# Third mixer: token parts behind the rotations and the last pair's copies first; first mixer: compression weights in a place of their own

## The chip, the core and the metric

The kernel runs on one core of a Trainium2 chip. The metric is the device time of one execution in microseconds (us). Engines are named as in the profile: PE is TensorE (PEld its weight loads), DVE is VectorE, ACT is ScalarE, POOL is GpSimd, and SP is the sync engine, which issues the DMAs.

## What is computed

Two transformer layers with modulated norms, then a third block of another make, on one sequence of 256 tokens and width 1024, all in float32:

```python
for layer in range(2):
    shift, scale, gate = split(c @ mod_w[layer, 0] + mod_b[layer, 0], 3)
    h = rms_norm(x, w) * (1 + scale) + shift
    y = mixer_ab(h, ...) if layer % 2 == 0 else mixer_cd(h, ...)
    x = x + gate * rms_norm(y, w)
    ...                                   # the same around swiglu(h, w_in, w_out)
# first mixer (ab), NSA part: compressed keys and values
kc = einsum('bnlgd,lde->bnge', k_cmp[:, gidx] + cmp_pe, cmp_wk)
vc = einsum('bnlgd,lde->bnge', v_cmp[:, gidx] + cmp_pe, cmp_wv)
# ... compressed, selected and window attention, weighed by gates; and a sliding window attention with sinks
# third mixer (sb): attention with rotated q, k and a token MLP, side by side
attn = block_attention(rope(rmsnorm(q)), rope(rmsnorm(k)), v)
tok = u * (einsum('hpq,bcqhd->bcphd', w_s, rmsnorm(v_tok)) + b_s)
mixed = concatenate([rmsnorm(attn, g_attn_out), rmsnorm(tok, g_tok_out)])
x = x + gt1 * (mixed @ w_out)             # then a gated FFN with a 3-tap convolution, and a last norm
```

## The kernel before

The program is written out engine by engine, with semaphores between the engines; nothing schedules it but the order of the code. The activations lie transposed (features on the 128 partitions, 256 tokens along the row). Every product of a weight with activations is made of three matmuls of fp32r, on the high and low parts of both operands (`three`, L1990 to L1992): high by high, low by high, high by low. For that each weight **unit** of 128x1024 is loaded to `raw` (SP, `load_unit`, L650), its high part is written by ACT to `wH` (`split_high`, L810) and its low part by DVE to `wL` (`split_low`, L1276), in rings of six slots. Beside this DVE makes the modulation vectors (`do_job`, L627 and L629): one **product** per modulation tile of 128x1024, which SP loads to `modbuf` (`load_job`, L660). In the first mixer a tile may be loaded once the product two before it is done (`mod_used`).

The stages in order: start, first mixer (ab, to about 180 us), FFN f0, second mixer (cd), FFN f1, third mixer (sb, 740 to 837 us), FFN f2, last norm.

**First mixer.** After the projections of keys and values, a loop of 15 steps `s` runs on SP, ACT, DVE and PE, each with its own list. In steps 0 to 11 PE makes the scores of two heads (`ab_scores`, L2332, L2335). DVE adds the bias and takes the minimum (`ab_neg`, L1629, L1631), ACT takes the exponential (`ab_exp`, L1005, with sinks L1010 from step 8). One step later DVE makes the factors of the rows (`ab_weigh`, L1639 to L1646) and scales the later two thirds of each head's probabilities (L1651), ACT scales the first third (L1018); this is "the weighing of step s - 1". Then PE turns the probabilities (`ab_turn`, L2347), ACT copies them out of PSUM (`ab_take_pt`, L1025), PE multiplies them with the values (`ab_pv`, L2364, L2367), ACT takes the high part of the finished features (`ab_features_high`, L1034) and DVE the low part (`ab_features_low`, L1657). The heads are numbered b = 2s and 2s + 1. In each step PE also does one projection (`ab_project`), from step 9 on one or two output products of 24 matmuls (`ab_out`).

The NSA compression runs in steps 0 and 1: `compress` (L2277 for the keys, L2280 for the values) multiplies windows with the weights `cw`, which lie in `otok` (1 MB on chip). Key and value weights share that place, so SP waits for the key product before it loads the value weights (L714). In step 5 PE turns the compressed probabilities (L2455), ACT copies them to `pcT` (L1084), and PE waits for that copy before it turns head 9. The hot matmul for the compressed bias (`misc["bc"]`, L2402) reads `hot_cmp`, in `proj` 9 to 12, at about 49 to 50 us; those tiles of `proj` are written with projections from step 4 on. `acc0[:, 2D:3D]` is written by the products from step 9 on.

**Third mixer.** The attention runs in four pairs of heads: `rope(n)` rotates a tile (L1822 to L1829), `pair_scores` (L2602), `pair_max` (L1837), `exp_pair` (L1161), `pair_turn` (L2617), then the two copies out of PSUM, the first head's by DVE (`copy_first`, L1848) and the second head's by ACT (`copy_second`, L1173), then `pair_pv` (L2631). Both copies count on one semaphore, `pt_ready`, and `pair_pv` waits for both. Scores of pair t need rotation t + 1. The token half is split into high and low parts by `mix_high` (ACT, L1183) and `mix_low` (DVE, L1877), which `token_out` reads, four units later.

```python
            def pair_pv(t):                                # L2625, PE
                pe.wait_ge(pt_ready, 32 + 2 * t + 2)
...
            def copy_first(t):                             # L1842, DVE
...
                V.tensor_copy(pt[:, 0, :], bank[2][:, :]).then_inc(pt_ready, 1)
```

## Time and profile before

| what | value |
|---|---|
| three runs | 1047.26, 1046.67, 1045.31 us; median 1046.67 |
| profiled execution | 1044.85 us, of it 1043.1 us from the first to the last instruction |
| PE busy | 994.2 us (95%), 8118 matmuls |
| DVE busy | 793.6 us (76%) |
| ACT busy | 560.4 us (54%) |
| mean granted clock of PE | 0.985 |
| read from HBM | 225.04 MB |

PE is nearly always busy, so its idle stretches are few and can be listed one by one. Matmuls are pipelined, so the time of one (0.28 us) is longer than the distance between two (about 0.12 us at the full clock). An idle stretch is shown in brackets behind the instruction that ended it, with what released it. The granted clock is a share of 2.4 GHz.

### The profile page before, as it was taken

The numbers are of one execution on the slowest core, as the hardware profiler recorded it, in microseconds if no ns is written. First come the engines' busy times: TensorE is split into PE (matmuls) and PEld (weight loads), VectorE is DVE, ScalarE is ACT, GpSimd is POOL, SyncE is SP. The second block draws the span as 40 slices with busy tenths as digits, with TensorE's granted clock in tenths as the row PEclk, the third lists the DMA queues.
The fourth block names the chain that finished last, engine by engine and source line by source line (L and its number), as shares of the span: only waits on it lengthen the run. The fifth ranks groups of instructions, "written<-read, shape, count | busy, mean of one in ns | idle before, by whom it ended". The sixth has DMA issues, their size and how long they took to land. (4 is left out here: it accounts for less than half of the span.)

```text
span 1043.1 us, 21347 instructions
## 1 busy us (share of the span) xinstructions
PE 994.2 (95%) x8118; PEld 959.4 (92%) x8118; DVE 793.6 (76%) x1320; ACT 560.4 (54%) x1126; POOL 4.6 (0%) x14
## 2 busy tenths in 40 slices
PE   6999989999999999999999999999998999999995
PEld 5997768899999999989899999998988989999995
DVE  4757875798888777888778888877766758777775
ACT  2444764544444456564454444446656456776664
POOL 0100000000000000000000000000000000000000
PEclk9998998999999999999999999999998999999999
DMA  9967767288888665832648888775612325455531
GB/s 356 344 206 226 248 220 265 88 328 309 301 301 304 248 252 174 300 118 74 230 181 304 304 301 302 284 263 177 246 66 74 126 98 182 181 186 187 188 144 42
DMA packets 62409, 227.59 MB, mean 218 GB/s; under 512 B 7010, under 2 KB 7266, under 8 KB 61956
## 3 DMA queue, kind: packets, MB, share of 16 engines
q1 hardware_dynamic: 61556, 224.02, 59.7%
q0 software_dynamic: 640, 2.10, 0.8%
q8 instruction: 47, 0.77, 0.3%
q10 hardware_dynamic: 144, 0.52, 0.1%
q14 instruction: 22, 0.18, 0.1%
HBM read 225.04 MB, written 1.57 MB: 217 GB/s over the span
## 5 line engine op out<-in xcount | busy, mean ns | idle before, releaser
L1990 PE MATMUL bank<-hH,wH 128*128 128x258 f32 (+1 forms) x1544 | 444.5, 288 | 11.1 <-DVE hL L1341 8.1
L1991 PE MATMUL bank<-hL,wH 128*128 128x258 f32 (+1 forms) x1544 | 438.2, 284 | 0.0
L1992 PE MATMUL bank<-hH,wL 128*128 128x258 f32 (+1 forms) x1544 | 436.6, 283 | 0.0
L1276 DVE TENSOR_TENSOR wL<-raw,wH 128x1024 fp32r<-128x1024 f32 x270 | 328.1, 1221 | 44.7 <-ACT wH L810 43.5
L1990 PEld LDWEIGHTS bank<-hH,wH 128*128 128x128 f32 x1544 | 292.7, 190 | 19.2 <-issue 10.6
L810 ACT ACTIVATE wH<-raw 128x1024 fp32r<-128x1024 f32 x270 | 276.6, 1047 | 43.5 <-PE bank L1992 25.1
L1992 PEld LDWEIGHTS bank<-hH,wL 128*128 128x128 f32 x1544 | 293.9, 190 | 0.0
L1991 PEld LDWEIGHTS bank<-hL,wH 128*128 128x128 f32 x1544 | 293.4, 190 | 0.4
L1990 PE MATMUL bank<-aH,wH 128*128 128x256 f32 x592 | 170.6, 288 | 3.0 <-DVE wL L1276 3.0
L1991 PE MATMUL bank<-aL,wH 128*128 128x256 f32 x592 | 169.7, 287 | 0.0
L1992 PE MATMUL bank<-aH,wL 128*128 128x256 f32 x592 | 169.6, 287 | 0.0
L1990 PEld LDWEIGHTS bank<-aH,wH 128*128 128x128 f32 x592 | 115.9, 196 | 4.2 <-DVE wL L1276 3.2
L1991 PEld LDWEIGHTS bank<-aL,wH 128*128 128x128 f32 x592 | 115.9, 196 | 0.0
L1992 PEld LDWEIGHTS bank<-aH,wL 128*128 128x128 f32 x592 | 115.7, 195 | 0.0
L930 ACT ACTIVATE fcol<-bank 128x1 f32<-128x1 f32 x132 | 15.2, 166 | 136.5 <-PE bank L1992 136.4
L1508 DVE TENSOR_TENSOR sn<-bank,rstd 128x256 f32<-128x256 f32 x44 | 18.7, 425 | 51.7 <-ACT fcol L930 51.7
L962 ACT ACTIVATE aH<-sn 128x256 fp32r<-128x256 f32 x66 | 27.5, 417 | 48.9 <-PE bank L1992 25.0
L629 DVE SCALAR_TENSOR_TENSOR acc<-modbuf,par,acc 128x1024 f32<-128x1024 f32 x28 | 35.9, 1281 | 10.0 <-DMA modbuf<-in_mod_w 9.2
L1528 DVE SCALAR_TENSOR_TENSOR pr<-sq,par,pr 128x255 f32<-128x255 f32 x44 | 19.4, 481 | 29.9 <-ACT pr L948 29.9
L935 ACT ACTIVATE sn<-sn,fcol 128x256 f32<-128x256 f32 x44 | 22.4, 510 | 28.2 <-DVE sn L1508 28.2
L856 ACT ACTIVATE hH<-x,sc 128x256 fp32r<-128x256 f32 x40 | 18.6, 502 | 23.8 <-DVE x L1385 17.2
L944 ACT ACTIVATE sq<-sq,fcol 128x256 f32<-128x256 f32 x44 | 20.1, 503 | 21.0 <-DVE sq L1519 21.0
(351 smaller groups left out, 1144.0 us busy)
## 6 DMA issues: line engine op xcount, KB each, us to landing
raw<-in_weights SPq DMA_DIRECT2D x270, 512.0 KB, 4.6
modbuf<-in_mod_w SPq DMA_DIRECT2D x69, 512.0 KB, 6.1
modbuf<-in_w_ada SPq DMA_DIRECT2D x36, 512.0 KB, 6.2
strips<-in_mod_w SPq DMA_DIRECT2D x16, 512.0 KB, 7.1
strips<-in_w_ada SPq DMA_DIRECT2D x12, 512.0 KB, 6.9
strips<-bias_table POOLq DMA_DIRECT2D x8, 256.0 KB, 7.2
otok<-in_cmp_w SPq DMA_DIRECT2D x4, 512.0 KB, 8.7
raw<-in_mod_w SPq DMA_DIRECT2D x2, 512.0 KB, 5.0
```

What stands on the lines that cost most here:

```text
L629: ops.scalar_tensor_tensor(out=dst, in0=src, scalar=cc[:, k:k + 1], in1=dst, op0=ALU.mult, op1=ALU.add).then_inc(mod_used, 1)
L810: nc.scalar.activation(wH[:, slot, :], raw[:, slot, :], ACT.Copy).then_inc(hi_ready[c], 1)
L856: nc.scalar.activation(hH[:, k, 0:S], x[:, k, :], ACT.Copy, scale=sc1[:, a, k:k + 1]).then_inc(hH_ready, 1)
L935: nc.scalar.activation(sn[:, t % 2, 0:S], sn[:, t % 2, 0:S], ACT.Silu, bias=fcol[:, t % 2, 0:1]).then_inc(silu_ready, 1)
L944: last = nc.scalar.activation(z, z, ACT.Identity, bias=fcol[:, t % 2, n:n + 1])
L962: nc.scalar.activation(aH[:, t % 2, :], sn[:, t % 2, S:2 * S], ACT.Copy).then_inc(aH_ready, 1)
L1276: V.tensor_tensor(wL[:, slot, :], raw[:, slot, :], wH[:, slot, :].bitcast(F32), ALU.subtract).then_inc(lo_ready[c], 1)
L1508: V.tensor_tensor(sn[:, t % 2, 0:S], gate_bank[:, 0:S], rstd[:, :], ALU.mult).then_inc(g_scaled, 1)
L1528: chain.inc(V.scalar_tensor_tensor(out=dst[:, 1:S], in0=z[:, 0:S - 1], scalar=row[:, 4 * n:4 * n + 1], in1=dst[:, 1:S], op0=ALU.mult, op1= ...
L1990: mm(out, lhs_h, rhs_h, start=start, stop=False, skip_group_check=True)
L1991: mm(out, lhs_h, rhs_l, start=False, stop=False, skip_group_check=True)
L1992: return mm(out, lhs_l, rhs_h, start=False, stop=stop, skip_group_check=True)
```

## The change

In words:

- First mixer, weights: the value weights are no longer loaded to `otok` behind the key product, but in two halves to `proj` 9 to 12 and to `acc0[:, 2D:3D]`, four DMAs of 256 KB on SP's queue after a wait for the bias product, ahead of units 12 and 13. `compress` waits for 96 in place of 64 and reads the halves. 
- First mixer, ACT: the copy to `pcT` in step 5 goes ahead of the split and the exponentials; in steps 9 to 12 the split goes ahead of the copy `ab_take_pt(2s - 2)`.
- First mixer, DVE: a step ends with one product less where it had two, and the other one comes in the next step right behind the weighing, ahead of the low part and the scores.
- Third mixer: `mix_high` 0 and 1 go behind the two roots `qk_rs` 3 and 4, `mix_low` 0 and 1 behind the rotations 3 and 4 and the maximum of pair 2. The last pair's copies go ahead of a split on either engine. The two copies count on a semaphore each (`turned_copied`), and the products of each head wait for its own.

```diff
@@ build_program
+        cw_values = [t.rearrange("p (l e) -> p l e", e=HD)
+                     for t in (proj[:, 9:13, :].rearrange("p a s -> p (a s)"), acc0[:, 2 * D:3 * D])]
+        turned_copied = [sem(f"turned_copied{j}") for j in range(2)]
@@ SP
             jobs_upto(JOBS_END["start"] + 2)
+            sp.wait_ge(misc_psum, misc["bc"] + 1)
+            for n in range(2):
+                for g in range(G):
+                    sp.dma_start(cw_values[n][g * HD:(g + 1) * HD],
+                                 A["cmp_w"][1][:, n * CLEN // 2:(n + 1) * CLEN // 2]).then_inc(cw_landed, 16)
             for p in range(12, 14):
                 load_unit(p)
             for s in range(AB_STEPS):
-                if s == 1:
-
-                    sp.wait_ge(misc_psum, misc["cmpk"] + 1)
-                    for g in range(G):
-                        sp.dma_start(cw[g * HD:(g + 1) * HD], A["cmp_w"][1]).then_inc(cw_landed, 16)
@@ ACT, first mixer
                     ab_weigh(s - 1)
+                if s == 5:
+                    act.wait_ge(pcT_psum, 1)
+                    nc.scalar.activation(pcT, bank[3][:, 0:S].rearrange("p (q n) -> p q n", q=QT),
+                                         ACT.Copy).then_inc(pcT_ready, 1)
...
+                split_upto(ab_split(s))
                 if 9 <= s <= 12:
                     ab_take_pt(2 * s - 2)
-                split_upto(ab_split(s))
...
-                if s == 5:
-                    act.wait_ge(pcT_psum, 1)
-                    nc.scalar.activation(pcT, bank[3][:, 0:S].rearrange("p (q n) -> p q n", q=QT),
-                                         ACT.Copy).then_inc(pcT_ready, 1)
@@ ACT, third mixer
             qk_unit(4)
-            mix_high(0)
-            mix_high(1)
             qk_rs(3)
             copy_second(1)
             qk_rs(4)
+            mix_high(0)
+            mix_high(1)
             exp_pair(2)
             copy_second(2)
             split_upto(base + 17)
             exp_pair(3)
-            split_upto(base + 18)
             copy_second(3)
             split_upto(base + 20)
@@ DVE, first mixer
                     ab_weigh(s - 1)
+                    jobs_upto(ab_jobs(s - 1))
...
-                jobs_upto(ab_jobs(s))
+                jobs_upto(min(ab_jobs(s), ab_jobs(s - 1) + 1) if 1 <= s <= 11 else ab_jobs(s))
@@ DVE, third mixer
-            mix_low(0)
-            mix_low(1)
             rope(3)
             copy_first(1)
             rope(4)
             pair_max(2)
+            mix_low(0)
+            mix_low(1)
             copy_first(2)
             pair_max(3)
             mod_take("modG5")
+            split_upto(base + 16)
+            copy_first(3)
             split_upto(base + 17)
-            copy_first(3)
@@ PE
             def compress(name, n):
-                pe.wait_ge(cw_landed, 32 * (n + 1))
+                pe.wait_ge(cw_landed, 32 if n == 0 else 96)
...
-                        w, x_ = cw[r, l, :], win[r, l, 0:NCMP]
+                        w = cw[r, l, :] if n == 0 else cw_values[2 * l // CLEN][r, l % (CLEN // 2), :]
+                        x_ = win[r, l, 0:NCMP]
@@ PE, pair_turn and pair_pv
-                    if j == 0 and t >= 1:
-                        pe.wait_ge(pt_ready, 32 + 2 * t)
+                    if t >= 1:
+                        pe.wait_ge(turned_copied[j], t)
...
-                pe.wait_ge(pt_ready, 32 + 2 * t + 2)
...
                 for j in range(2):
+                    pe.wait_ge(turned_copied[j], t + 1)
```

Where this moves instructions, the order on the engine says more than the diff. On DVE, first mixer, around the weighing in step 10 (L1645 to L1651 before; products are L629, the low part L1657, splits L1276), before:

```order
L1276 TENSOR_TENSOR wL<-raw,wH 128x1024
L627 TENSOR_SCALAR acc0<-modbuf,par 128x1024
L629 SCALAR_TENSOR_TENSOR acc0<-modbuf,par,acc0 128x1024
L1645 TENSOR_TENSOR sm<-sm,sinkx 128x4
L1646 RECIPROCAL sm<-sm 128x4
L1651 TENSOR_SCALAR sq<-sq,sm 128x256 x2
L1657 TENSOR_TENSOR aL<-bank7,aH 128x256
```

and in the changed kernel (all of its line numbers are two or three higher):

```order
L1278 TENSOR_TENSOR wL<-raw,wH 128x1024
L630 TENSOR_SCALAR acc0<-modbuf,par 128x1024
L1647 TENSOR_TENSOR sm<-sm,sinkx 128x4
L1648 RECIPROCAL sm<-sm 128x4
L1653 TENSOR_SCALAR sq<-sq,sm 128x256 x2
L632 SCALAR_TENSOR_TENSOR acc0<-modbuf,par,acc0 128x1024
L1659 TENSOR_TENSOR aL<-bank7,aH 128x256
```

One of two products has moved from ahead of the weighing to behind it, and so ahead of the low part. Steps 2, 3, 5, 6, 8, 9, 10 and 12 have such a product behind the weighing; steps 4, 7 and 11, whose step before has a single product, have none.

On DVE, third mixer, from the rotations to the last pair's copy (rotation L1822 to L1829, copies L1848, maximum L1837 and L1838, low parts L1877), before:

```order
L1877 TENSOR_TENSOR aL<-proj,aH 128x512 x2
L1822 TENSOR_TENSOR otok<-bank,con 128x256
L1823 TENSOR_TENSOR proj<-proj,con 128x256
L1829 TENSOR_TENSOR proj<-proj,otok 128x256
L1848 COPY pt<-bank 128x512
...
L1329 COPY gw<-mv 128x8
L1276 TENSOR_TENSOR wL<-raw,wH 128x1024 x2
L1848 COPY pt<-bank 128x512
L1454 RECIPROCAL rg<-sm 128x16
L1276 TENSOR_TENSOR wL<-raw,wH 128x1024
```

and in the changed kernel:

```order
L1840 TENSOR_REDUCE nm<-bank 128x2
L1841 SCALAR_TENSOR_TENSOR nm<-nm,qrs 128x2
L1880 TENSOR_TENSOR aL<-proj,aH 128x512 x2
L1851 COPY pt<-bank 128x512
...
L1331 COPY gw<-mv 128x8
L1278 TENSOR_TENSOR wL<-raw,wH 128x1024
L1851 COPY pt<-bank 128x512
L1278 TENSOR_TENSOR wL<-raw,wH 128x1024
L1456 RECIPROCAL rg<-sm 128x16
L1278 TENSOR_TENSOR wL<-raw,wH 128x1024
```

The two low parts now stand behind the maximum of the third pair and ahead of its copy, and the last pair's copy stands between two splits instead of behind both.

On SP, the loads around the value weights (`otok` and `acc` / `proj` as their places), before:

```order
L650 DMA raw<-in_weights 128x1024 x4
L660 DMA modbuf<-in_mod_w 128x1024 x2
L650 DMA raw<-in_weights 128x1024 x3
L714 DMA otok<-in_cmp_w 64x2048 x2
L650 DMA raw<-in_weights 128x1024
L660 DMA modbuf<-in_mod_w 128x1024 x2
```

and in the changed kernel:

```order
L653 DMA raw<-in_weights 128x1024 x4
L663 DMA modbuf<-in_mod_w 128x1024 x2
L713 DMA proj<-in_cmp_w 64x1024 x2
L713 DMA acc<-in_cmp_w 64x1024 x2
L653 DMA raw<-in_weights 128x1024 x4
L663 DMA modbuf<-in_mod_w 128x1024 x2
```

The weights have moved ahead of three units, and the fourth unit and the modulation tiles no longer stand behind them.

## Rows read from the trace of the kernel before

**Rows 1.** The page: busy time of the engines, and the granted clock in 40 slices.

```profile
PE 994.2 (95%) x8118; PEld 959.4 (92%) x8118; DVE 793.6 (76%) x1320; ACT 560.4 (54%) x1126; POOL 4.6 (0%) x14
...
PEclk9998998999999999999999999999998999999999
```

**Rows 2.** Timeline, PE, first mixer: start us, us, instruction, [idle before, releaser].

```profile
84.25 3.75 PE L2280 MATMUL bank<-otok,pt 64*15 64x64 f32 x128 [0.93 <-DMA otok<-in_cmp_w]
...
93.23 0.48 PE L2448 MATMUL bank<-vcs,con 15*128 15x128 f32 x2 [0.51 <-DVE vcs L1693]
...
98.46 0.88 PE L2347 MATMUL bank<-con,pr 128*128 128x128 f32 x6 [0.39 <-ACT pr L1018]
...
113.98 0.55 PE L2347 MATMUL bank<-con,pr 128*128 128x128 f32 x3 [2.46 <-ACT pt L1084]
...
136.05 0.55 PE L2347 MATMUL bank<-con,pr 128*128 128x128 f32 x3 [1.82 <-ACT pr L1018]
...
157.99 0.90 PE L2347 MATMUL bank<-con,sq 128*128 128x128 f32 x3 [2.73 <-ACT sq L1018]
...
159.10 1.12 PE L2364 MATMUL bank<-pt,vt 128*64 128x256 f32 x4 [0.21 <-DVE hL L1657]
```

**Rows 3.** Timeline, PE and DVE, third mixer, rotations to the last pair.

```profile
787.53 1.29 DVE L1877 TENSOR_TENSOR aL<-proj,aH 128x512 fp32r<-128x512 f32 x2 [1.54 <-ACT aH L1183]
...
790.00 1.13 PE L2602 MATMUL bank<-proj 64*128 64x256 f32 x8 [1.30 <-DVE proj L1829]
...
798.94 2.36 DVE L1276 TENSOR_TENSOR wL<-raw,wH 128x1024 fp32r<-128x1024 f32 x2
...
801.96 3.06 PE L2631 MATMUL bank<-vt,pt 128*128 128x64 f32 x16 [1.09 <-DVE pt L1848]
```

**Rows 4.** Windows: stretch, its length, busy us (instructions) per engine, PEclk, DMA share, GB/s.

```profile
76.50:83.30 6.80, 6.80 (x40) 5.92 (x38) 2.68 (x11) 1.87 (x8) 0.00 (x0) 0.56 0.76 171
100.40:103.80 3.40, 3.40 (x21) 2.62 (x20) 3.26 (x11) 2.77 (x10) 0.00 (x0) 0.63 0.48 172
137.90:141.40 3.50, 3.50 (x21) 3.50 (x21) 2.16 (x3) 3.32 (x12) 0.00 (x0) 0.63 0.64 245
158.40:165.20 6.80, 6.59 (x35) 5.56 (x34) 3.44 (x4) 2.48 (x4) 0.00 (x0) 0.56 0.69 245
803.50:810.30 6.80, 6.80 (x37) 6.80 (x37) 5.13 (x7) 2.18 (x7) 0.00 (x0) 0.56 0.40 143
...
165.20:172.00 6.80, 6.80 (x59) 6.35 (x58) 5.65 (x6) 3.04 (x5) 0.00 (x0) 1.00 0.77 283
```

**Rows 5.** SP's issue of the value weights, landing times of modulation tiles, and a full DMA window.

```profile
76.92 1.11 SPq L714 DMA_DIRECT2D otok<-in_cmp_w  x2
...
DMA to landing us min/median/max: 3.3/4.5/10.0
...
56.00:62.00 6.00, 6.00 (x46) 5.63 (x46) 1.28 (x2) 3.22 (x5) 0.00 (x0) 1.00 1.03 378
```

**Rows 6.** Timeline, DVE, first mixer: products and one low part.

```profile
87.96 2.67 DVE L629 SCALAR_TENSOR_TENSOR acc<-modbuf,par,acc 128x1024 f32<-128x1024 f32 x2 [6.72 <-DMA modbuf<-in_mod_w]
...
115.42 1.28 DVE L629 SCALAR_TENSOR_TENSOR acc<-modbuf,par,acc 128x1024 f32<-128x1024 f32 x1 [1.06 <-DMA modbuf<-in_mod_w]
...
132.60 2.67 DVE L629 SCALAR_TENSOR_TENSOR acc<-modbuf,par,acc 128x1024 f32<-128x1024 f32 x2
...
143.72 0.42 DVE L1657 TENSOR_TENSOR aL<-bank,aH 128x256 fp32r<-128x256 f32 x1 [0.38 <-ACT aH L1034]
```

**Rows 7.** Timeline, ACT, first mixer: the copy of step 5 and one of step 9.

```profile
113.56 0.36 ACT L1084 ACTIVATE pt<-bank 128x256 f32<-128x256 f32 x1
...
137.66 0.49 ACT L1025 ACTIVATE pt<-bank 128x384 f32<-128x384 f32 x1 [1.38 <-PE bank L2367]
```

**Rows 8.** Windows of the first mixer's steps 2 to 8, and of its end.

```profile
91.60:135.20 43.60, 39.27 (x310) 31.23 (x308) 40.29 (x118) 32.02 (x102) 0.00 (x0) 0.96 0.67 228
157.10:177.70 20.60, 19.50 (x141) 18.02 (x142) 13.00 (x18) 8.50 (x13) 0.00 (x0) 0.83 0.74 276
```

More of the change, by code:

```diff
@@ L1172, in copy_second @@
                     act.wait_ge(pv_done, a - 1)
-                nc.scalar.activation(pt[:, 1, :], bank[3][:, :], ACT.Copy).then_inc(pt_ready, 1)
+                nc.scalar.activation(pt[:, 1, :], bank[3][:, :], ACT.Copy).then_inc(turned_copied[1], 1)
             def tok_square(t):
@@ L1847, in copy_first @@
                     dve.wait_ge(pv_done, a)
-                V.tensor_copy(pt[:, 0, :], bank[2][:, :]).then_inc(pt_ready, 1)
+                V.tensor_copy(pt[:, 0, :], bank[2][:, :]).then_inc(turned_copied[0], 1)
             def token_mixed(t):
@@ L2693, in _ @@
             pair_pv(3)
-            pe.wait_ge(pt_ready, 40)
+            for j in range(2):
+                pe.wait_ge(turned_copied[j], 4)
             for i in range(4):
```

## The prediction

> **What bounds the kernel now.** I read the page first. TensorE (PE) is busy for 994.2 of 1043.1 us, VectorE (DVE) for 793.6 and ScalarE (ACT) for 560.4, and the granted clock is full in all but a few slices [rows 1]. PE is the path; a change can give back only what PE idles and what it does at the low clock. Then I read PE's timeline in the two stages that the diff touches. In the steps of the first mixer (84 to 160 us) PE stands still for 0.93, 0.51, 0.39, 2.46, 1.82, 2.73 and 0.21 us [rows 2] and three times more, for 0.24, 0.47 and 0.56: together 10.3 us. In the third mixer the idle stretches that the edits reach are 1.30 us before the third pair's scores and 1.09 us before the last pair's products [rows 3]. Last the windows: five stretches have a mean granted clock of 0.56 to 0.63, which is 1.2 GHz for most of the window and 2.4 GHz at its edges [rows 4]. In the stretch from 158.4 PE gets through 35 matmuls, in the 6.8 us behind it through 59 [rows 4], so a stretch of 6.8 us costs (59 - 35) / 59 x 6.8 = 2.8 us and one of 3.4 us half of that, 1.4.
>
> **The change part by part.**
>
> *Compression weights.* Before, SP issued the value weights at 76.92 us [rows 5], once PE had read the key weights, and a weight unit and two modulation tiles stood behind that wait in its queue. PE waited 0.93 us for the weights [rows 2], and DVE stood idle for 6.72 us, since its tiles came only at 87.96 [rows 6]. Now four loads of 256 KB (1 MB) go to `proj` 9 to 12 and `acc0`, issued behind the bias product (about 50 us), ahead of units 12 to 14. The 0.93 goes. The cost is DMA time: the queue is full there, and 1 MB at the 378 GB/s of 56 to 62 us [rows 5] is 2.8 us by which units 12 to 14 land later. What waits for them on ACT and DVE ends in probabilities that PE does not turn before 87.9 us, some 19 us behind the split of unit 12, so that hides it; without that cover it would cost up to 2.8. DVE gains more than PE: its two products run at about 81.3 and 83.5, and the step after begins at 88.4 in place of 91.6. That takes the 0.51 and the 0.39 as well.
>
> *Copy of the turned compressed probabilities* (ACT, step 5). It stood behind a split and four exponentials, and PE waited 2.46 us for it [rows 2, 7]. Now two short scalings are ahead of it. About 0.9 us of waiting are left here, and PE is 5.1 us ahead behind it.
>
> *One modulation product behind the weighing* (DVE). A pair of products took 2.67 us directly ahead of the weighing for which PE waited 1.82 us [rows 2, 6]; one of them, 1.3 us, now comes behind it. The work per step stays, and DVE now holds PE. From 91.6 to 135.2 us DVE is busy for 40.3 of 43.6 us [rows 8]; the same work from 88.4 on, less the product that moves behind the weighing, with 1.2 us of waiting for the repeated values and 1 to 2 of short waits, brings the weighing of step 8 to 129.7 to 131.5 us against 135.2. PE is ready for it at 134.2 - 5.1 = 129.1 and needs the first scaled part, 0.9 us later: it waits 1.5 to 3.3 us, and I take 2.3. The product is also ahead of the low part now (0.42 us, with its wait of 0.38 for ACT [rows 6]). PE waits for that part: about 0.5 us at step 10 and 1.4 us at step 12.
>
> *Split ahead of the copy* (ACT, steps 9 to 12). The copy waits for PE (1.38 us at 137.66 [rows 7]) and held the split and the exponentials behind it, and DVE stood behind them for 1.2 to 1.6 us a step. This goes. The copy's own reader is a turn behind 3.1 us of output products, so that its delay by one split costs nothing.
>
> *Sum of the first mixer.* Of 10.3 us idle, 5.2 come back (0.1 + 0.9 + 2.3 + 0.5 + 1.4): 5.1 gained. The three low stretches at 100.4, 137.9 and 158.4 cost 1.4 + 1.4 + 2.8 = 5.6. With all of them gone the gain is 10.7. With all there it is 7.5, since of the first two only 0.4 counts: PE would wait for DVE at steps 8 and 10 anyway. Behind the last weighing DVE has 13.0 us of work [rows 8] and now some 19 us for it, so nothing is given back there.
>
> *Third mixer.* DVE's two low parts (1.29 us) stood ahead of the rotation for which PE waited 1.30 us [rows 3], and ACT's two high parts ahead of the root that the rotation needs. Both move behind. The 1.30 goes, and the parts fit in where DVE waits for PE's turns. The last pair's copy stood behind two splits of 2.36 us [rows 3]; with one of them behind it, PE waits about 0.3 us in place of 1.09. That is 2.1 us. The low stretch at 803.5 costs 2.8 [rows 4]. If it goes, DVE's splits and the attention half's low parts get late by some 0.8: 4.1 in all, or 2.1 with the clock as it is. The separate semaphores let the first head's products start before the second copy; the copies end within 0.3 us of each other, so I take nothing more.
>
> *The clock.* The ends are 10.7 + 4.1 = 14.8 us, if the four low stretches go (the one at 76.5 follows the small compression products, which stay), and 7.5 + 2.1 = 9.6, if none goes. No row shows which: idle of 2.46 us was not followed by a low stretch, idle of 1.82 us was [rows 2, 4]. I take the middle, 12.2. For tiles that land late I take off 0.8: one such wait cost 1.06 [rows 6], landing takes 4.5 us in the median and 10.0 at most [rows 5], and the ends are 0 and 3.
>
> By the Trainium skill (TensorE: Matmul & The Clock Gate, "Why this matters for your kernels") a drop of the clock takes a gap between bursts that is longer than any idle stretch here, so that closing these would give back no clock. The trace does not bear that rule out, since low stretches follow gaps of 1.82 and 2.73 us and even follow no gap at 76.5. What the rule would make of the time is rival 1.
>
> **The number.** 12.2 - 0.8 = 11.4 us. The profiled execution took 1044.85 us (span 1043.1) and would take 1033.4. The median of the three runs is 1046.67, so I forecast 1035.3. About 0.2% (2 us) is what a measurement of this kernel can tell from no change.
>
> **Rivals.**
> 1. *The clock stays as low as before*, in these places or in others. For it: the stretch at 76.5 comes with no idle ahead, and new idle of over 2 us is left at step 8. Against it: the idle stretch of 2.73 us ahead of the longest one goes. Gain 9.6 - 0.8 = 8.8, time 1037.9.
> 2. *DVE takes back more.* For it: DVE is busy almost without a break from 91.6 to 135.2 [rows 8], and most steps have a product ahead of the low part. If it holds PE at every step as at step 12, the first mixer gives the 0.93 and about 2.0 of the copy's wait, and the third its 2.1: 5.0 us, time 1041.7.
> 3. *The edits do not do what they say*: the idle moves on to the next wait of the same step in full. Gain under 2 us, time 1045.5. Against it: each wait named has one instruction or load ahead of it that leaves.
> 4. *Slower: the tiles of the second products land late.* A product's load starts when the product two before is done, about 4.9 us before it is due (seven steps in the 43.6 us of [rows 8] are 6.2 us each, less 1.3). With landings of L us, eight steps wait 8 x (L - 4.9). From L = 6.4 on this eats the 12.2 us; at 7 us it is 16.8 - 12.2 = 4.6 slower, 1051.3. For it: 10.0 us has been seen, and DMA is at 0.5 to 0.8 in these steps. Against it: the median is 4.5, and the loads that made it long have left this stretch.
>
> **How the numbers follow.** Forecast, with the clock partly back: 0.52. Rival 1: 0.24. Rival 2: 0.14. Rival 3: 0.06. Rival 4: 0.04. The range goes from the full 14.8 us, 1031.9, with 0.4 more for a step 8 that waits only 1.5 us, 1031.5, to rival 2 with late tiles, 0.8 more, 1042.5; rivals 3 and 4 and a part of the others are left out. Faster by over 2 us are the first three, 0.90; the same is rival 3, 0.06; slower is rival 4, 0.04.
>
> **What would show it.** PE no longer waits for the value weights, and DVE uses the tiles of 87.96 at 81 to 84. PE's idle at step 5 is under 1 us. At step 8 PE waits 1.5 to 3.3 us for the weighing, at step 12 about 1.4 for the low part. PE ends the output products of step 12 eight to eleven us before 168.5. In the third mixer the 1.30 is gone and the 1.09 is about 0.3. Of the low stretches at 137.9, 158.4 and 803.5 some are gone. I am wrong if DVE waits for tiles in several steps, if PE waits over 4 us at step 8, or if the stages outside the two mixers change by more than 1 us.

## The result, and the profile after

| | before | changed | |
|---|---|---|---|
| first comparison, median | 1046.51 us (4 runs) | 1030.12 us (4 runs) | ratio 0.9845, 95% interval 0.9826 to 0.9863 |
| all runs of the study | mean 1047.4, 1042.6 to 1053.0 (65 runs) | mean 1030.3, 1027.9 to 1033.3 (13 runs) | 17.1 us |
| mean granted clock in them | 0.9852, 0.979 to 0.991 | 0.9933, 0.991 to 0.995 | |
| profiled execution (span) | 1044.85 (1043.1) | 1031.67 (1029.8) | 13.2 us |

The forecast was 1035.3 with a range of 1031.5 to 1042.5: the right sign and the right places, but the gain is 16 to 17 us where 11.4 were forecast, and the time is 1.4 us below the range. Two things stand in the table already. The clock rose: no run of the changed kernel lies below the best of before. And the profiled execution of before was faster than the three runs shown with it and than nearly all of the later ones, that of the changed kernel was the slowest of its four.

The page of the changed kernel, busy times and granted clock (before: [rows 1]):

```profile
PE 987.3 (96%) x8118; PEld 954.4 (93%) x8118; DVE 792.3 (77%) x1320; ACT 559.9 (54%) x1126; POOL 4.6 (0%) x14
...
PEclk9999999999999999999999999999999999999998
```

PE's timeline in the first mixer: the rows that answer to [rows 2] and each idle stretch of over 0.5 us.

```profile
83.19 1.96 PE L2285 MATMUL bank<-proj,pt 64*15 64x64 f32 x64
...
91.61 0.48 PE L2453 MATMUL bank<-vcs,con 15*128 15x128 f32 x2
...
107.27 1.18 PE L2352 MATMUL bank<-con,pr 128*128 128x128 f32 x6
...
128.40 0.49 PE L2337 MATMUL bank<-proj 64*128 64x128 f32 x4 [0.67 <-DVE nm L1633]
...
131.36 0.55 PE L2352 MATMUL bank<-con,pr 128*128 128x128 f32 x3 [2.04 <-ACT pr L1021]
...
138.75 0.65 PE L2369 MATMUL bank<-pt,vt 128*64 128x256 f32 x4 [0.89 <-DVE aL L1659]
...
145.00 0.65 PE L2369 MATMUL bank<-pt,vt 128*64 128x256 f32 x4 [0.56 <-DVE hL L1659]
...
150.14 0.55 PE L2352 MATMUL bank<-con,sq 128*128 128x128 f32 x3 [0.87 <-ACT sq L1021]
...
151.28 0.65 PE L2369 MATMUL bank<-pt,vt 128*64 128x256 f32 x4 [0.59 <-DVE hL L1659]
```

The value weights, the step behind them and the copy of step 5 hold PE no longer; what is left is the wait of step 8 and the short ones behind it, 5.8 us with one of 0.18, where it was 10.3. In the third mixer the two waits of [rows 3] are gone. These are the third pair's scores, the last pair's products, and the one new wait, which DVE's low parts end (PE's rows):

```profile
783.99 1.14 PE L2607 MATMUL bank<-proj 64*128 64x256 f32 x8
...
789.10 2.00 PE L2636 MATMUL bank<-vt,pt 128*128 128x64 f32 x16
...
806.09 0.36 PE L1994 MATMUL bank<-hH,wH 128*128 128x256 f32 x1 [0.76 <-DVE hL L1880]
```

Windows of the changed kernel (columns as in [rows 4]): the low stretch at 76.5 is there as before; the three shown with 1.00 are at the full clock, as is all between 83 and 1013 us (the work of 158.4 to 165.2 is now at about 150.5 to 155, that of 803.5 at about 791); a low stretch that the trace of before doesn't have lies near the end, at 1015.3. The wait ahead of it, 2.96 us for the last unit's low part, is in both traces, and of the 16 traces of the study that have this wait 12 have a low stretch behind it.

```profile
76.50:83.30 6.80, 6.80 (x48) 5.97 (x48) 6.49 (x22) 4.26 (x17) 0.00 (x0) 0.59 0.67 228
100.40:103.80 3.40, 3.40 (x35) 2.88 (x33) 3.37 (x13) 3.21 (x10) 0.00 (x0) 1.00 0.73 240
...
153.00:159.80 6.80, 6.80 (x59) 6.35 (x58) 5.26 (x6) 3.04 (x5) 0.00 (x0) 1.00 0.93 336
793.00:799.80 6.80, 6.80 (x59) 6.80 (x58) 6.58 (x8) 3.96 (x8) 0.00 (x0) 1.00 0.31 103
1015.30:1022.10 6.80, 6.68 (x29) 5.86 (x28) 4.78 (x12) 2.52 (x4) 0.00 (x0) 0.60 0.00 0
```

PE's timeline gives the account between the two profiled executions. The stage behind the first mixer begins at 186.72 before and at 176.55 now: 10.2 us, which is 4.5 of idle (10.3 to 5.8) and the 5.6 of the three low stretches. From there to the third mixer both take 566.6 us. The third mixer (with the first norm sums behind it) takes 96.9 before and 92.5 now: 4.4 us, of which 1.3 is idle (1.30 + 1.09 - 0.76, and 0.3 more at 822.74, where 0.90 became 1.20) and 2.8 the price of the low stretch at 803.5; 0.3 is left over. The rest takes 1.4 us longer with its low stretch at 1015.3. 14.6 - 1.4 = 13.2.

So of the four low stretches that the prediction put a price on none is left. Theory A: idle makes them, and closing the idle takes them away. Theory B: which stretch is low is chance from one execution to the next, and the edits give only their idle. Theory C, for the parts alone: DVE and ACT set the steps, and PE waits in the next place for what it gained.

### The profile page after: what moved, and what is told of

It reads as the page before. It is cut to its first block and busy times, and to the rows that moved or that the text cites. A ratio compares the mean times of both kernels' runs of the same rounds, so it can differ in the third digit from the quotient of the medians.

```text
span 1029.8 us, 21353 instructions
## 1 busy us (share of the span) xinstructions
PE 987.3 (96%) x8118; PEld 954.4 (93%) x8118; DVE 792.3 (77%) x1320; ACT 559.9 (54%) x1126; POOL 4.6 (0%) x14
## 5 line engine op out<-in xcount | busy, mean ns | idle before, releaser
L859 ACT ACTIVATE hH<-x,sc 128x256 fp32r<-128x256 f32 x40 | 18.6, 502 | 22.8 <-DVE x L1387 17.1
```

The lines of the kernel that those rows point to most:

```text
L859: nc.scalar.activation(hH[:, k, 0:S], x[:, k, :], ACT.Copy, scale=sc1[:, a, k:k + 1]).then_inc(hH_ready, 1)
```

## Each part alone, on the kernel before

Four kernels, each with one part of the diff: the weights (`cw_values`, SP's four loads, `compress`); DVE's products; ACT's two moves in the first mixer; the third mixer.

> The kernel before with the value weights in their own place, and nothing else of the change. Both theories: the 0.93 us idle ahead of the value compression goes, the 0.51 and 0.39 behind it as well, and DVE's two tiles of 87.96 us are used at 81 to 84. Theory A (the clock follows the idle: each closed idle stretch takes the low stretch behind it away): the low stretch at 100.4 goes too, 1.8 + 1.4 = 3.2 us faster than before. Theory B (the clock's low stretches come by chance, the edits give their idle alone): 1.8 us. Theory C (DVE and ACT set the steps from 91 us on, PE only waits more at steps 5 and 8): under 1 us.

> The kernel before with one modulation product behind the weighing, and nothing else of the change. Both: the 1.82 us idle at step 8 shrinks to 0.5, since one product of 1.3 us leaves the place ahead of it. Theory A: the low stretch at 137.9 goes as well, 1.3 + 1.4 = 2.7 us. Theory B: 1.3 us. Theory C: the time is given back at step 12 (idle 2.73 us there grows to 4), 0 us.

> The kernel before with ACT's two moves in the first mixer alone (copy of step 5 ahead of split and exponentials; split ahead of the copy in steps 9 to 12). Both: the 2.46 us at step 5 shrink to about 0.9, PE then waits 1.5 us longer at step 8 (3.3 us), where DVE holds it; at step 12 the 2.73 us shrink to 1.3. Theory A: the low stretch at 158.4 goes too: 1.4 + 2.8 = 4.2 us. Theory B: 1.4 us. Theory C: under 1 us.

> The kernel before with the third mixer's part alone. Both: the 1.30 us ahead of the third pair's scores goes and the 1.09 us ahead of the last pair's products shrinks to 0.3 or less. Theory A: the low stretch at 803.5 goes too: 2.1 + 2.8 = 4.9, less up to 0.8 for low parts that come late, 4.1 us. Theory B: 2.1 us. The first mixer is as before, with its low stretches at 100.4, 137.9 and 158.4 under A.

| part alone | runs | median us | ratio to before (1046.83), 95% | mean clock | gain |
|---|---|---|---|---|---|
| weights | 12 | 1044.54 | 0.9955 to 0.9985 | 0.9858 | 2.3 |
| products | 6 | 1040.66 | 0.9920 to 0.9959 | 0.9903 | 6.2 |
| ACT's moves | 12 | 1046.15 | 0.9964 to 1.0000 | 0.9848 | 0.7 |
| third mixer | 12 | 1044.01 | 0.9961 to 0.9984 | 0.9875 | 2.8 |

The sum is 12.0 us, 5 short of the whole. The medians carry much chance, though: by the ratios the four give 14.3 us, with some 3.4 of uncertainty (from the four intervals), against 16.3 (mean of the whole's three ratios, 0.9844). So it isn't shown that the parts fall short of the whole. PE's timeline shows what an edit leaves. With the weights alone step 5 has more idle than before:

```profile
108.58 0.55 PE L2350 MATMUL bank<-con,pr 128*128 128x128 f32 x3 [1.05 <-ACT pr L1020]
111.84 0.55 PE L2350 MATMUL bank<-con,pr 128*128 128x128 f32 x3 [2.71 <-ACT pt L1086]
136.91 0.90 PE L2350 MATMUL bank<-con,pr 128*128 128x128 f32 x3 [1.79 <-ACT pr L1020]
...
159.72 0.55 PE L2350 MATMUL bank<-con,sq 128*128 128x128 f32 x3 [2.74 <-ACT sq L1020]
```

The wait for the weights is gone, but 1.05 and 2.71 stand where before had 2.46. The kernel with the third mixer's part alone, which still loads the weights the old way, has 1.06 and 2.71 there too, so the edit didn't bring them: PE is 1.5 us ahead of that kernel at step 5 (111.84 against 113.37) and level with it at step 8 (136.91 against 136.97), and its low stretch between the two is 6.8 us long, the other's 3.4. With ACT's moves alone idle does go from step 5 to step 8 (3.3 us expected there, 3.42 measured):

```profile
110.86 1.11 PE L2347 MATMUL bank<-con,pr 128*128 128x128 f32 x6 [1.10 <-ACT pr L1018]
...
136.22 0.55 PE L2347 MATMUL bank<-con,pr 128*128 128x128 f32 x3 [3.42 <-ACT pr L1018]
...
156.38 0.55 PE L2347 MATMUL bank<-con,sq 128*128 128x128 f32 x3 [1.43 <-ACT sq L1018]
```

and with the products alone step 8 is down to 0.45 us, and its low stretch is not there. The windows behind these waits, first of the kernel with the weights alone:

```profile
113.60:120.40 6.80, 6.80 (x33) 5.50 (x33) 6.06 (x20) 4.34 (x14) 0.00 (x0) 0.54 0.81 294
137.50:140.90 3.40, 3.40 (x20) 2.46 (x19) 0.97 (x7) 1.52 (x3) 0.00 (x0) 0.58 0.82 282
161.40:164.80 3.40, 3.40 (x22) 2.91 (x18) 0.90 (x1) 2.37 (x3) 0.00 (x0) 0.58 0.92 343
```

then of the kernel with the products alone (behind 3.58 us of idle at 113.4, and behind 1.32 and 1.29 at 155.7 and 157.5):

```profile
114.20:117.60 3.40, 3.40 (x18) 1.80 (x16) 2.30 (x5) 1.99 (x6) 0.00 (x0) 0.57 1.02 399
158.60:162.00 3.40, 3.40 (x18) 3.40 (x19) 1.94 (x2) 2.38 (x3) 0.00 (x0) 0.57 0.89 347
```

The low stretches lie behind idle, as theory A says. The times decide less. The products' interval (4.3 to 8.4 us) lies above all three theories (2.7, 1.3, 0), and why they gave so much was not shown. ACT's moves (0 to 3.8) leave out A's 4.2, but C's under 1 isn't told from B's 1.4. Weights (1.6 to 4.7) and third mixer (1.7 to 4.1) allow both A and B. In the kernel with the third mixer alone that stage has no low stretch. Its first mixer, the same program as before's, has low stretches at 76, 138 and 158 again, but one at 114 and none at 100.4. No other kernel with the old loading has one at 100.4 either: of six traces only that of before does.

## The clock alone

`c_fill` is the kernel before with nothing moved but PE's waits around the fills. While PE waits, it works on constants; the records show each product twice.

```diff
             def ab_turn(b):
+                if b == 16:
+                    pe.wait_ge(proj_done, 12)
+                    fill(bank[5], 7)          # 7 products of ident with ones
+                if b == 22:
+                    pe.wait_ge(neg_ready, 24)
+                    fill(bank[0], 11)
...
             def pair_scores(t):
+                if t == 2: fill(bank[0], 5)
...
             def pair_pv(t):
+                if t == 3: fill(bank[0], 4)
```

> The kernel before, with nothing moved: while PE waits (step 8 1.82 us, step 12 2.73, third pair's scores 1.30, last pair's products 1.09) it makes 7, 11, 5 and 4 products of constants that nobody reads. Theory A: the low stretches behind these places (137.9, 158.4, 803.5) go, the mean clock rises by 0.007, and the time falls by up to 1.4 + 2.8 + 2.8 = 7.0 us, less up to 1 us where the last fill ends late. Theory B: clock and time as before, or up to 1 us slower.

Measured: 1042.52 us (5 runs) against 1047.48, ratio 0.9938 to 0.9965, 5.0 us faster; the mean clock is 0.9924 in place of 0.985, a rise of 0.0075. That is nearly the 0.0081 of the whole change. The fills and, from the windows, the three places of [rows 4] that they were meant for:

```profile
135.83 1.83 PE L2340 MATMUL bank<-con 128*128 128x128 f32 x14
...
156.62 2.62 PE L2340 MATMUL bank<-con 128*128 128x128 f32 x22
```

```profile
137.90:141.40 3.50, 3.50 (x31) 3.02 (x31) 2.10 (x9) 2.30 (x8) 0.00 (x0) 1.00 0.86 291
158.40:165.20 6.80, 5.97 (x50) 5.32 (x49) 3.80 (x8) 3.63 (x7) 0.00 (x0) 1.00 0.87 290
803.50:810.30 6.80, 6.80 (x59) 6.80 (x58) 6.20 (x8) 3.46 (x8) 0.00 (x0) 1.00 0.39 133
```

All three are at 1.00, with 50 matmuls (a few of them fills) where there were 35, and 59 where there were 37. Theory B falls: work without any use, at the place of the wait, brings the clock back, and time with it. The other idle stretches were left alone, and behind two of them this kernel has low stretches (behind 3.90 us ahead of the value weights, and behind 2.71 at step 5). 2 of the 7 us expected did not come; how much of them the ends of the fills cost was not separated.

Rival 1 of the prediction falls with this.

## Each part taken out of the changed kernel

> The changed kernel with one of its moves undone: in steps 9 to 12 ACT's split is behind the copy again. Idle of PE at step 12 goes from 0.87 back to about 2.7 us. Theory A (the low stretches follow the idle): a low stretch of 3.4 to 6.8 us comes back near 152, mean clock 0.989 to 0.991, the time 1.9 + 1.4 to 1.9 + 2.8 = 3.3 to 4.7 us above the changed kernel. Theory B (which stretch is low is chance): clock unchanged at 0.993, 1.9 us slower.

> The changed kernel with both products ahead of the weighing again, as in the kernel before. Idle of PE at step 8 goes from 2.04 to 3.3 us, and the short waits for the low parts (0.6 to 0.9) go. Theory A: a low stretch comes back behind step 8 and another behind step 12, the mean clock falls by 0.003, and the time rises by 1.3 - 0.9 + 2.8 = 3.2 us. Theory B: clock unchanged, 0 to 0.5 us slower. It was the one part that alone raised the clock of the kernel before.

> The changed kernel with the value weights loaded as before (behind the key product, in one place). PE waits 0.9 to 3.9 us for them again, DVE begins step 2 some 3 us later and holds PE at step 8. If the parts only add: 2.3 us slower than the changed kernel (what the part gave alone). If DVE's early start is what the other edits build on: 4 to 6 us slower, with 2 to 4 us of idle at step 8 and a low stretch behind it.

> The changed kernel with the third mixer as before. By the stage times of the traces it takes 96.8 or 100.1 us there in place of 92.5: 4.4 to 7.6 us slower than the changed kernel, mean clock 0.987 to 0.990. By the part alone on the kernel before: 2.8 us slower.

```diff
 u_split, ACT:
-                split_upto(ab_split(s))
                 if 9 <= s <= 12:
                     ab_take_pt(2 * s - 2)
+                split_upto(ab_split(s))
 u_products, DVE:
-                    jobs_upto(ab_jobs(s - 1))
...
-                jobs_upto(min(ab_jobs(s), ab_jobs(s - 1) + 1) if 1 <= s <= 11 else ab_jobs(s))
+                jobs_upto(ab_jobs(s))
```

`u_weights` and `u_third` are the change without its hunks for the weights and for the third mixer.

| taken out | runs | median us | mean clock | slower than the changed kernel (1030.1) | ratio to before, 95% (changed: 0.9831, 0.9845, 0.9855) |
|---|---|---|---|---|---|
| split ahead of the copy | 6 | 1035.19 | 0.9905 | 5.1 | 0.9838 to 0.9895 |
| one product behind the weighing | 6 | 1036.63 | 0.9897 | 6.5 | 0.9858 to 0.9906 |
| weights | 4 | 1033.79 | 0.9925 | 3.7 | 0.9860 to 0.9898 |
| third mixer | 4 | 1034.74 | 0.9912 | 4.6 | 0.9873 to 0.9911 |

The four come to 19.9 us (with the copy of step 5 still in). But these runs and those of the changed kernel were not made side by side. By the ratios to the runs of before beside them (0.9866, 0.9882, 0.9879, 0.9892, against 0.9844) they come to 2.3, 4.0, 3.7 and 5.0, together 15.0. One figure lies above the whole and one below it, so it isn't shown that the parts need each other. For the first two, where the figures differ most, the runs of before were slow (median 1048.37); `v4`, made beside them, was not (1027.70, see below), which speaks for the medians. The split's 5.1 us is above theory A's 3.3 to 4.7, its 2.3 near B's 1.9; the clock decides for A: it falls into the range that A gave, and four of the six runs (0.988 to 0.990) lie below all 13 of the changed kernel. In the profiled execution of it, at 0.993, the first mixer has no low stretch behind the one at 76. The products give 6.5 or 4.0, where 3.2 was expected. In the trace without them step 8 has 3.42 us of idle, and low stretches follow behind steps 8 and 12. Without the weights' own place PE waits 1.77 us at the value weights, and then 0.85 and 1.47 for low parts; step 8 has the 2.04 us as before. So DVE is later, but the wait that comes of it lies at the low parts, not at the weighing, and there is no low stretch behind it. The third mixer's part is worth 4.4 to 7.6 us by the stage times of the traces before this run and 4.6 measured; its 2.8 alone on the kernel before, 12 runs, stays a little short of that, and why was not settled.

That stage (to the wait of 1.35 us for a low weight part just behind it) is also where a single trace misled. It takes 96.9 us in the trace of before. In four other kernels with the old order it takes 100.1, 96.8, 100.1 and 95.3 us (weights, products, ACT's moves alone, and `u_third`), in `c_fill`, old order with filled waits and no low stretch, 94.2, and 92.4 to 92.5 in all twelve traces with exactly the change's order. The windows of the kernel with ACT's moves alone show the difference: two low stretches where [rows 4] has one.

```profile
790.30:797.10 6.80, 6.80 (x37) 6.59 (x38) 1.19 (x3) 2.51 (x9) 0.00 (x0) 0.57 0.00 0
804.00:810.80 6.80, 6.80 (x38) 6.80 (x38) 4.45 (x7) 2.26 (x7) 0.00 (x0) 0.58 0.44 155
```

Behind the same two waits (1.30 and 1.09 us) one execution has a low stretch of 3.4 us, others 6.8, others twice 6.8, so how much comes differs between executions; that some comes doesn't, in these: all five have one, and none of the twelve.

## The changed kernel again, and beyond it

> The changed kernel again, more runs of it. Theory A (the clock follows the idle): the mean granted clock stays at 0.992 to 0.995 in every run, above all runs of the kernel before (0.982 to 0.991 in 29), and the time is 1028.5 to 1032, 16 us below the kernel before. Theory B (chance): some runs at 0.985 to 0.988 and 1036 to 1039 us, as the kernel before has runs 10 us apart.

Measured 1030.08 us (1027.9 to 1032.2, 5 runs), clock 0.991 to 0.995, ratio 0.9812 to 0.9849: theory A, though one run is at 0.991. The best run of before in clock (0.991) meets the worst of these; in time there are 9 us between the fastest run of before and the slowest of the changed kernel.

`v1` puts DVE's low part ahead of the product behind the weighing; `v2` spreads the products differently on top of it.

```diff
 v1, DVE:
                     ab_weigh(s - 1)
-                    jobs_upto(ab_jobs(s - 1))
                 for f in range(8):
                     if AB_FT_STEP[f] == s - 1:
                         ab_features_low(f)
+                if 1 <= s <= 12:
+                    jobs_upto(ab_jobs(s - 1))
 v2, ab_jobs:
-            return min(JOBS_END["ab"], JOBS_END["start"] + (24 * (s + 1) + 13) // 14)
+            return JOBS_END["start"] + (2, 4, 5, 6, 8, 9, 10, 12, 14, 16, 18, 20, 22, 24, 24)[s]
```

> The changed kernel with DVE's low part ahead of the product that came behind the weighing. If this product holds PE at the low part (waits of 0.89 at 138.75, 0.56 at 145.0 and 0.59 at 151.28 us), these go: up to 1.5 us faster than the changed kernel. If DVE is the bound of steps 2 to 8 and ACT's weighing (0.87 at 150.14) that of the later ones, the waits move to the next weighing: no difference.

> As v1, with the modulation products spread differently: two fewer before the weighing of step 8 (14 in place of 16 at that step's end), two in each of steps 7 to 13. If DVE's work bounds PE up to step 8, the 0.67 and 2.04 us there go: 2.0 to 2.7 us faster than the changed kernel with v1's part, and DVE's products behind step 12 end later, with 6 us of slack. Rival: the tiles land late, or two products a step hold the weighing of steps 9 to 12 (two at 1.3 us each): the idle moves there, no gain.

`v1`: 1031.25 us, no gain. In its trace the wait at the first low part is 0.21 (0.21 to 0.89 in the changed kernel's three), and a new one of 0.39 comes at the next turn: the wait moves to the weighing. `v2`: 1028.67 us against 1030.08, intervals of the ratios 0.9797 to 0.9826 and 0.9812 to 0.9849, which overlap: 1.4 us where 2.0 to 2.7 were expected, and not clear of noise. The trace supports a gain: the wait for the scores' minimum is gone and that of step 8 is halved.

```profile
129.64 0.54 PE L2353 MATMUL bank<-con,pr 128*128 128x128 f32 x3 [1.04 <-ACT pr L1021]
```

So DVE's amount of work ahead of step 8 is what is left there, as the prediction said of its 2.3 us.

`i_keys` is `v2` with the small compression products spread between the matmuls of projections 8 and 9.

```diff
 PE, steps 0 and 1:
-                        ab_project(e)
...
-                    compress("cmpk" if s == 0 else "cmpv", s)
+                        ab_project(e, lambda k: compress("cmpk" if s == 0 else "cmpv", s, k))  # an eighth behind each k
```

> v2 with the 128 small products of the compression (64x64 by 64x15) spread between the eight thirds of projections 8 and 9 instead of in one block of 4 us. The low stretch that every kernel has at 76.5 to 78 comes without idle ahead. If it comes from the block of small products, it goes: up to 2.8 us faster than v2 and the clock 0.003 higher. If it comes from something else (the place in the run, transfers), it stays and the time is as v2's. If small products cost more between large ones (another weight size each time), slower by up to 1 us per block.

Measured 1036.28 us, 7.6 slower than `v2`. The low stretch at 76.5 is not in its trace, and one of 6.8 us begins at 81, in a new wait of 1.95 us: the value products now begin before DVE has taken the keys' result. And the mix is dear. These rows are 1.12 us apart, in which 16 small products and 3 large ones are made:

```profile
70.92 0.64 PE L2288 MATMUL bank<-pt,otok 64*64 64x15 f32 x16
72.04 0.64 PE L2288 MATMUL bank<-pt,otok 64*64 64x15 f32 x16
73.16 0.64 PE L2288 MATMUL bank<-pt,otok 64*64 64x15 f32 x16
```

In `v2` the projection takes 3.05 us and the block 4.09, an eighth of both is 0.89. If both blocks pay the same, that is 3.7 us of the 7.6, and the wait is 1.95; where the rest went was not shown. Whether the stretch at 76.5 hangs on the block of small products isn't shown. The trace points to it, but `c_fill` and `u_third` have the block in one piece and no low stretch there either: 16 of the 18 traces with the block have one, and one trace without it can be the chance of those two. A gain by spreading isn't shown either.

`v4` and `v5` are `v2` and take on two waits that the change leaves: 0.77 us in the third mixer, and 2.95 us in the last stage, where PE waits for the last unit's low part:

```diff
 v4 and v5, last step of the last stage; ACT, and DVE likewise:
+                        if t == FT - 1:
+                            split_high(base + 3 * t + 2)
                         act.wait_ge(conv_ready, at(t + 1, 2))
...
-                    if t >= 2:
+                    if t >= 2 and (phase != "f2" or t < FT - 1):
                         split_high(base + 3 * t + 2, i)
 v4 only, DVE, third mixer:
-            split_upto(base + 22)
+            split_upto(base + 20)
...
             mix_low(3)
+            split_upto(base + 22)
 v6 only, PE, on top of v5 (and fill of 7 and 8 in ab_turn 16 and 22, as in c_fill):
+                    keep_clock(bank[4], 14)
                 down(FT - 1)
```

> v2, and two more edits of the same kind as the change's: in the third mixer DVE's splits 20 and 21 behind the scaling of the attention half and its low parts (wait of 0.77 at 804.5 goes), and in the last stage's last step the split of the last unit on ACT and DVE ahead of the gate, where both stand idle (PE waits 2.95 us at 1013 for that low part; the low part of the activations, 1.2 us later than PE is there, is next). Both theories: 0.77 + 1.7 = 2.5 us faster than v2. Theory A: the low stretch behind the 2.95 us goes too, or gets shorter, 1 to 2 us more. If the splits hold PE in their new place: no gain.

> v2 with the last stage's edit alone (last unit's split ahead of the gate), the third mixer as in the changed kernel. v4's 2.09 us at 820.9 is 1.20 again, the last stage's idle is 1.8 in place of 2.95. 1.1 us faster than v2, about 1027.3, 2.5 to 3 us faster than the changed kernel. If v4's low stretch at 822 came with its 2.09 us, it is not here.

> The changed kernel once more, beside v5 and v6 on the same chip: 1030 us, mean clock 0.993 to 0.994.

> v5 with products of constants in the idle stretches of step 8 (7), step 12 (8) and of the last stage (14). If idle of 1.0 to 1.8 us still lowers the clock now and then, the mean clock rises by 0.001 to 0.002 and the time falls by 1 to 2 us; if not, clock and time as v5's, or up to 0.5 us slower where a fill ends late.

`v4`: 1027.70 us, 1.0 below `v2` where 2.5 were expected. PE's timeline of it has the 0.77 gone and a longer wait behind it, at the first matmul of the last stage; in the last step 1.81 is left.

```profile
820.86 0.39 PE L1998 MATMUL bank<-hH,wH 128*128 128x258 f32 x1 [2.09 <-DVE hL L1345]
...
1013.28 0.36 PE L1998 MATMUL bank<-aH,wH 128*128 128x256 f32 x1 [1.81 <-DVE aL L1554]
```

The third mixer and the first norm sums behind it take 94.0 us in place of 92.5: that edit fails, the splits hold DVE later, and a low stretch of 3.4 us lies behind the 2.09, which `v5` doesn't have. `v5`, without it: 1025.18 us (1024.8 to 1028.9, 5 runs), ratio to before 0.9785 to 0.9815. The changed kernel on the same chip (`after3`): 1030.62, 0.9834 to 0.9875. These two intervals don't meet, so `v5` beats both kernels, by about 4 us (means 1026.3 and 1030.3) and 21 us. `v6` fills what idle is left in steps 8 and 12 and in the last stage: 1028.20 us, 0.9794 to 0.9827, mean clock 0.9956 against `v5`'s 0.9954. In the profiled executions `v5` has low stretches of 3.4 us behind 1.24 and 1.79 us of idle (at 149.9 and 1013.5), and `v6` has none there. So the fills may still keep the clock, but in five runs each no gain of time is seen.

## Why the prediction was off

**What held.** The mechanism is the forecast's, place by place. At the value weights and the 0.51 and 0.39 behind them: 0 left. Step 5: 0.9 expected, 0 measured. Step 8: 2.3 expected, 2.04 measured. Step 10: 0.5 and 0.89. Step 12: 1.4 and 0.87 + 0.59 = 1.46. Third mixer: the 1.30 gone; the 1.09 expected at 0.3, measured at 0; the late low part expected at 0.8, measured at 0.76. The output products of step 12 end 10.2 us earlier (eight to eleven). Not foreseen were 0.67 at the scores of step 9 and 0.56 at a low part, 1.2 together. Late tiles: DVE waits over 1 us for one only once (1.42 us), 0.8 was taken off, and rival 4 fails with that; the two tiles of 87.96 are used at 81.62 and 84.28. Nothing changed between the mixers. Two sums of the text don't come out of its terms: PE's lead at step 8 is 4.8 by them (0.93 + 0.51 + 0.39 + 1.56 + 1.4) where it has 5.1 (4.9 measured), and the weighing of step 8 at 129.6 to 130.6 where it has 129.7 to 131.5. With the text's 129.1 and 0.9 that is a wait of 1.4 to 2.4, which the 2.04 us fit better than the 2.3 taken.

**The step that failed** is "I take the middle, 12.2": the clock's term was halved, 2.6 of 5.2 us, without a row that speaks for the half. In the traces of the pair all four low stretches that had a price are gone. The full sum of the text, 14.8 less 0.8 for tiles, is 14.0 us, and the stages of the two traces give 14.6. The reason for the middle was that no row showed whether low stretches follow the idle. The count of rows was too thin for that: 2.46 us without and 1.82 us with a low stretch behind it are two draws. Over the traces of the study 1.78 to 1.82 us at step 8 was followed by one in three of three, 2.5 to 3.6 at step 5 in four of five, the third mixer's pair of waits in five of five, but the changed kernel's 2.04 us at step 8, in seven traces of kernels that have it, only twice. So whether a stretch comes differs from place to place and from execution to execution, and that new idle of 2 us at step 8 mostly stayed without one is luck as far as the prediction goes.

**The second fault was in the base**, not in the change. The prediction priced the low stretches of one execution and put that price on the median. This execution was 2.2 us below the median of the 65 runs (1047.06). In the third mixer it had one low stretch where two of five had two, and its wait of 0.93 us for the value weights was 1.1 to 3.9 in the five other kernels with the old loading. Worked from the runs instead: a low stretch of 6.8 us costs 2.8 us and lowers the mean clock by 0.5 x 6.8 / 1043 = 0.0033, so 0.001 of clock is 0.85 us. The clock's 0.0081 is 6.9 us, and the other 10.2 of the 17.1 are waits. The same rule makes 6.5 and 6.7 of the 13.2 between the two profiled executions: the clock's part agrees, and the waits' part is 3.5 us larger in the runs than in the one pair of traces. The stages of the other traces say where the 3.9 us between the pair (13.2) and the runs (17.1) lie. The first mixer ends at 186.7 and 187.7 us in the two traces that have all of it as before (before and the third mixer's part alone), and at 174.7 to 176.6 in the four that have it as changed (`after`, `after2`, `after3`, `u_third`): 11.7 us between the means, in place of the pair's 10.2. The later of the two has 12.7 us of idle where before has 10.3: 2.23 for the value weights, and 1.06 and 2.71 at step 5. The third mixer takes 97.8 in the mean of five traces and 92.5 as changed: 5.3 in place of 4.4. And the last stage's low stretch, 1.4 against the changed kernel in the pair, is one that either kernel can have. 11.7 + 5.3 = 17.0, an estimate from few traces, agrees with the runs.

**The range** had its lower end at the full 14.8 us plus 0.4, which holds for the profiled pair. It left out that the base itself was one execution, 2.2 us from the median of the runs.

## What to carry to other kernels

Where PE is the bound and traces show a low clock behind its waits, price such a wait with the low stretch behind it, not only with its idle time: here that was 40% of the gain. Size alone doesn't tell which waits: 1.2 to 1.4 us at the start of the third mixer and behind it was followed by none in all 19 traces, 1.09 to 1.30 inside it by one in five of five. Count low stretches over several executions (the mean clock in the list of runs will do) before the price of one trace goes into a sum, and set the base by runs. Look at the waits of one stage together: ACT's moves alone made step 8 wait 3.42 us in place of 1.82, in the changed kernel, where the products' part is in as well, it is 2.04. And before two sums of parts are called different, compare their intervals: medians of 4 to 12 runs gave 12.0 and 19.9 us for the same four parts.

## What the runs showed of the chip

- Useless matmuls in the waits gave 5.0 us and 0.0075 of mean clock with no other edit. By the Trainium skill (TensorE: Matmul & The Clock Gate, "Why this matters for your kernels") only a longer pause between bursts does that harm; the measurement decides, and the idle stretches that were filled were 1.1 to 2.7 us long.
- The same program ran between 0.979 and 0.991 of mean clock in 65 runs and over 10 us of time; the fit through them is 0.82 us for 0.001 of clock, next to the 0.85 worked out from the windows.
- A block of 128 products of 15 columns is followed by a low stretch with no idle right ahead in 16 of 18 traces. In the one trace with the products spread among large matmuls it is absent, which doesn't show the cause. So mixed, 16 small and 3 large take 1.12 us in place of 0.89.
